# First block of a two-block model on one core: feed-forward part joined to the output projection, its row divisor applied to the products

## What is computed

```python
merged = g_a * (y_a @ w_o_rwkv) + g_b * (y_b @ w_o_att)
h = h + merged @ w_out

z = rmsnorm(h, norm2_g) @ w_ffn_in
z_gate, z_up = jnp.split(z, 2, axis=-1)
h = h + (jax.nn.silu(z_gate) * z_up) @ w_ffn_out
```

## Time and profile before

| | us |
|---|---|
| median of 3 runs | 1678.6 (1671.26 to 1678.84) |
| profiled execution, its own time | 1683.73 |
| its span in the trace | 1681.9 |

### The profile page before, as it was taken

One profiled execution on the slowest core, in us unless ns is written; L12 is line 12 of the kernel. 1 busy time (PEld: TensorE's weight loads), 2 busy tenths in 40 slices (PEclk: granted clock), 3 DMA queues, 4 the chain that ended last, 5 costly groups with the idle time before them and its releaser, 6 DMA issues. The chain is left out here.

```text
span 1681.9 us, 37220 instructions
## 1 busy us (share of the span) xinstructions
PE 1539.9 (92%) x15430; PEld 1247.0 (74%) x15430; DVE 923.8 (55%) x1100; ACT 761.4 (45%) x936; POOL 119.8 (7%) x66
## 2 busy tenths in 40 slices
PE   5998999988998969999999988889999898999996
PEld 4997877888998969999888778866555555555552
DVE  3487434355443356764500433566787676777774
ACT  2346216324442328732111324324676666666663
POOL 0321400001342000000300000000000000000000
PEclk8999999998999989999999999999999999999998
DMA  7556357542554525554022233447999999999992
GB/s 231 166 173 211 115 175 230 190 159 92 188 175 150 178 75 175 163 163 127 28 76 75 76 100 101 133 176 245 404 409 378 354 377 403 408 408 372 408 392 106
DMA packets 197323, 360.10 MB, mean 214 GB/s; under 512 B 12221, under 2 KB 140586, under 8 KB 197034
## 3 DMA queue, kind: packets, MB, share of 16 engines
q1 hardware_dynamic: 197162, 357.82, 60.0%
HBM read 355.03 MB, written 1.05 MB: 212 GB/s over the span
## 5 line engine op out<-in xcount | busy, mean ns | idle before, releaser
L350 PE MATMUL psum<-proj_r 128*128 128x256 f32 x1504 | 380.3, 291 | 34.5 <-DVE proj_r L335 18.7
L351 PE MATMUL psum<-proj_r 128*128 128x256 f32 x1504 | 377.7, 289 | 0.0
L319 DVE TENSOR_TENSOR ring_r<-ring,proj_r 128x2048 fp32r<-128x2048 f32 x94 | 220.6, 2346 | 209.6 <-ACT proj_r L314 208.8
L350 PEld LDWEIGHTS psum<-proj_r 128*128 128x128 f32 x1504 | 299.0, 199 | 38.8 <-issue 28.8
L351 PEld LDWEIGHTS psum<-proj_r 128*128 128x128 f32 x1504 | 298.9, 199 | 0.0
L2191 DVE COPY ring<-proj 128x2048 f32 x189 | 226.9, 1224 | 118.5 <-PE psum L2833 62.9
L314 ACT ACTIVATE proj_r<-ring 128x2048 fp32r<-128x2048 f32 x94 | 179.4, 1908 | 120.9 <-PE psum L354 120.6
L354 PE MATMUL psum<-proj_r,ring_r 128*128 128x256 f32 x1504 | 197.2, 284 | 2.7 <-DVE ring_r L319 2.6
L1661 ACT ACTIVATE ring<-proj 128x1024 f32 x188 | 191.3, 1050 | 14.4 <-issue 8.5
L354 PEld LDWEIGHTS psum<-proj_r,ring_r 128*128 128x128 f32 x1504 | 188.7, 193 | 3.1 <-DVE ring_r L319 3.1
L427 PE MATMUL psum<-u,ring 128*128 128x256 f32 x512 | 124.9, 390 | 6.1 <-ACT proj L1495 6.1
(11 more groups left out here) (495 smaller groups left out, 2256.2 us busy)
## 6 DMA issues: line engine op xcount, KB each, us to landing
ring<-in_w_in SPq DMA_DIRECT2D x65, 1024.0 KB, 5.3
proj<-in_w_exp_gate SPq DMA_DIRECT2D x128, 512.0 KB, 7.6
proj<-in_w_exp_up SPq DMA_DIRECT2D x128, 512.0 KB, 10.1
proj<-in_w_exp_down SPq DMA_DIRECT2D x128, 512.0 KB, 8.4
ring<-in_w_ada SPq DMA_DIRECT2D x24, 1024.0 KB, 7.8
ring<-in_w_ffn_in SPq DMA_DIRECT2D x22, 1024.0 KB, 5.1
ring<-in_w_ffn_out SPq DMA_DIRECT2D x11, 1024.0 KB, 4.9
ring<-in_w_out SPq DMA_DIRECT2D x8, 1024.0 KB, 4.9
```

What stands on the lines that cost most here:

```text
L319: dve.tensor_tensor(ring_r[:, at.slot, :], ring[:, at.slot, :], self.heads[at.buffer].bitcast(F32), ALU.subtract) \
L350: pe.matmul(dst, w, xh, start=start, stop=False, skip_group_check=True)
L351: pe.matmul(dst, w, xl, start=False, stop=False, skip_group_check=True)
```

## The change

- The barrier and the norm stage between output projection and feed-forward go. As soon as chunk 4 + i has added to two tiles of `h`, ACT copies their heads with the gain (`h * g`, not divided by the norm) and squares them, and DVE makes the rests (`head_of_pair`, `rest_of_pair`). The first feed-forward chunk is treated as a ninth chunk of the projection.
- PE sums the squares of a pair of tiles behind chunks 5, 6 and 7 and behind the first feed-forward chunk (`sum_of_pair`); that chunk waits for the rows' rests at four places in place of two.
- The divisor `rs`, one number per token, is applied to the products: DVE multiplies the gate product in PSUM by it (`scale_gate`), ACT applies SiLU in place in SBUF, DVE multiplies by the up product and then again by `rs` (`up_product`). Pair 0 lies in banks 1 and 3 and is written out ahead of the loop.
- Each pair therefore counts twice in `pair_evacuated`. PE asks for the pair two before its own in place of three.
- PE's 14 modulation turns move: 10 ahead of output chunk 0, 4 behind chunk 3.
- A down chunk waits for the split of its own pair alone.

Arguments such as `finished` are passed as functions; names of signals are renumbered to fit.

```diff
--- before.py
+++ after.py
@@ -344,8 +344,8 @@
             for i, (o, (xh, xl), dst, start, stop) in enumerate(products):
-                if halves and i in (0, len(products) // 2):
-                    pe.wait_ge(*reached("input_rests", halves[i > 0]))
+                if halves and i % (len(products) // len(halves)) == 0:
+                    pe.wait_ge(*reached("input_rests", halves[i * len(halves) // len(products)]))
...
@@ -960,9 +960,15 @@
                         act.activation(o.mix.xh[i], merged[:, 4 * i:4 * i + 4, :], ACT.Copy).then_inc(sig("input_heads"), 1)
+                if finished and c >= chunks - 2:
+                    finished(c - (chunks - 2), at(c - 2))
+            if finished:
+                o.mix.head(act, at(chunks))
+                finished(2, at(chunks - 2))
+                finished(3, at(chunks - 1))
...
-        def dve_out(dve, place, o, chunks, first_gated, write, early=0, gates=False):
+        def dve_out(dve, place, o, chunks, first_gated, write, early=0, gates=False, finished=None):
...
@@ -973,8 +979,10 @@
             for c in range(chunks):
-                if c + 1 < chunks:
+                if c + 1 < chunks or finished:
                     o.mix.rest(dve, at(c + 1))
+                if finished and c > chunks - 4:
+                    finished(c - 1 - (chunks - 4))
...
@@ -992,9 +1000,11 @@
                     write(c - (chunks - 4), at(c)).then_inc(evacuated, 1)
+            if finished:
+                finished(3)
...
-        def pe_out(pe, place, o, first_tiles, chunks):
+        def pe_out(pe, place, o, first_tiles, chunks, finished=None):
...
@@ -1009,6 +1019,8 @@
                 multiply_split(pe, sp_, at, products, halves)
+                if finished:
+                    finished(c - (chunks - 3))
...
@@ -1279,12 +1291,11 @@
             st.end()
-            st.end()
...
             for i in range(DFF // CH):
-                pool.wait_ge(*reached("pair_evacuated", i + 4))
-                pool_split(pool, *(flat_of(ap) for ap in (ffn_tmp[i % 3], ffn_h[:, 2 * i:2 * i + 2, :], ffn_l[:, 2 * i:2 * i + 2, :])))
+                pool.wait_ge(*reached("pair_evacuated", 2 * (i + 3)))
+                pool_split(pool, *(flat_of(ap) for ap in (ffn_tmp[(i + 2) % 3], ffn_h[:, 2 * i:2 * i + 2, :], ffn_l[:, 2 * i:2 * i + 2, :])))
...
@@ -1466,21 +1477,32 @@
             place.skip(8 - GATES_FIRST)
-            act_out(act, place, out_1, 8)
-            st.end()
-            act_norm(act, 1)
-            split_free.act_input(act, 1)
-            split_free.head(act, Chunk(place, 0, 0, None))
-            def silu_gate(at):
+            def head_of_pair(i, at):
+                act.wait_ge(evacuated, at.linear + 3)
+                for k in (2 * i, 2 * i + 1):
+                    ins = act.activation(split_free.tiles(k)[0], h[:, k, :], ACT.Copy, scale=v("norm2_g", k))
+                ins.then_inc(sig("input_heads"), 1)
+                act.activation(squares[:, 2 * i:2 * i + 2, :], h[:, 2 * i:2 * i + 2, :], ACT.Square).then_inc(sig("squares_act_1"), 1)
+            act_out(act, place, out_1, 8, finished=head_of_pair)
+            split_free.head(act, Chunk(place, 1, 1, None))
+            act.activation(small[:, 250:251], const("ones")[:, 0:1], ACT.Sqrt)
+            act.wait_ge(*reached("variance_1", 1))
+            act.activation(rs[:, :], rs[:, :], ACT.Sqrt).then_inc(sig("root_1"), 1)
+            split_free.head(act, Chunk(place, 2, 2, None))
+            def silu_gate(pair, buffer):
+                act.wait_ge(*reached("gate_steps", pair * 2 + 1))
+                act.activation(ffn_tmp[buffer], ffn_tmp[buffer], ACT.Silu).then_inc(sig("gate_steps"), 1)
+            def head_and_gate(at):
...
                 if at.j % 2 == 0:
-                    act.wait_ge(multiplied, at.n + 1)
-                    act.wait_ge(*reached("hid_split", at.pair + 1))
-                    src = bank[at.j // 2 % 3 * 2].rearrange("p (m t) -> p m t", t=S)
-                    act.activation(ffn_tmp[at.j // 2 % 3], src, ACT.Silu).then_inc(sig("gate_silu"), 1)
-            sweep(act, place, 2 * (DFF // CH), silu_gate, linear=False, split=True)
+                    silu_gate(at.pair + 1, at.j // 2 % 3)
+            silu_gate(0, 2)
+            place.skip(2, False, True)
+            sweep(act, place, 2 * (DFF // CH) - 2, head_and_gate, linear=False, split=True)
...
@@ -1868,14 +1890,45 @@
             two_tiles = lambda at: bank[2 * at.parity].rearrange("p (m t) -> p m t", t=S)
+            def rest_of_pair(i):
+                dve.wait_ge(*reached("input_heads", INPUTS_BEFORE["ffn"] + i + 1))
+                for k in (2 * i, 2 * i + 1):
+                    head, rest = split_free.tiles(k)
+                    ins = dve.scalar_tensor_tensor(out=rest, in0=h[:, k, :], scalar=v("norm2_g", k), in1=head.bitcast(F32), op0=ALU.mult, op1=ALU.subtract)
+                ins.then_inc(sig("input_rests"), 1)
+            dve.drain().then_inc(sig("pair_evacuated"), 4)
...
                     lambda c, at: dve.tensor_tensor(merged[:, 4 * c:4 * c + 4, :], wide_tiles(at), proj[:, T_GATE + 4 * c:T_GATE + 4 * c + 4, :], ALU.mult),
-                    lambda c, at: dve.tensor_tensor(h[:, 2 * c:2 * c + 2, :], two_tiles(at), h[:, 2 * c:2 * c + 2, :], ALU.add))
-            st.end()
-            dve.drain().then_inc(sig("pair_evacuated"), 3)
-            dve_norm(dve, link, 1, lambda k: v("norm2_g", k))
-            split_free.dve_input(dve, 1)
-            split_free.rest(dve, Chunk(place, 0, 0, None))
+                    lambda c, at: dve.tensor_tensor(h[:, 2 * c:2 * c + 2, :], two_tiles(at), h[:, 2 * c:2 * c + 2, :], ALU.add),
+                    finished=rest_of_pair)
+            by_token = rs[:, :].rearrange("p (o t) -> p o t", o=1).to_broadcast([P, 2, S])
+            def scale_gate(n, pair, buffer, src):
+                dve.wait_ge(multiplied, n)
+                dve.wait_ge(*reached("hid_split", pair + 1))
+                dve.tensor_tensor(ffn_tmp[buffer], src.rearrange("p (m t) -> p m t", t=S), by_token, ALU.mult).then_inc(sig("gate_steps"), 1)
+            def up_product(n, pair, buffer, src):
+                dve.wait_ge(multiplied, n)
+                dve.wait_ge(*reached("gate_steps", pair * 2 + 2))
+                dst = ffn_tmp[buffer]
+                dve.tensor_tensor(dst, dst, src.rearrange("p (m t) -> p m t", t=S), ALU.mult).then_inc(sig("pair_evacuated"), 1)
+                dve.wait_ge(*reached("pair_evacuated", pair * 2 + 5))
+                dve.tensor_tensor(dst, dst, by_token, ALU.mult).then_inc(sig("pair_evacuated"), 1)
+            first = [Chunk(place, j, j, None) for j in range(2)]
+            split_free.rest(dve, first[1])
+            dve.wait_ge(*reached("square_sum_1", 1))
+            dve.tensor_scalar(rs[:, :], bank[7][:, 0:S], 1.0 / D, 1e-6, ALU.mult, ALU.add).then_inc(sig("variance_1"), 1)
+            dve.wait_ge(*reached("root_1", 1))
+            link(dve.reciprocal(rs[:, :], rs[:, :]))
+            scale_gate(first[0].n + 1, 0, 2, bank[1])
+            split_free.rest(dve, first[1].after())
+            up_product(first[1].n + 1, 0, 2, bank[3])
+            place.skip(2, False, True)
...
@@ -1892,15 +1945,11 @@
-            def up_product(at):
+            def rest_and_pair(at):
                 split_free.rest(dve, at.after())
-                if at.j % 2 == 1:
-                    dve.wait_ge(multiplied, at.n + 1)
-                    dve.wait_ge(*reached("gate_silu", at.pair + 1))
-                    dst = ffn_tmp[at.j // 2 % 3]
-                    dve.tensor_tensor(dst, dst, bank[at.j // 2 % 3 * 2 + 1].rearrange("p (m t) -> p m t", t=S), ALU.mult) \
-                       .then_inc(sig("pair_evacuated"), 1)
-            sweep(dve, place, 2 * (DFF // CH), up_product, linear=False, split=True)
+                buffer = at.j // 2 % 3
+                (up_product if at.j % 2 else scale_gate)(at.n + 1, at.pair + 1, buffer, bank[(buffer + 2) % 3 * 2 + at.j % 2])
+            sweep(dve, place, 2 * (DFF // CH) - 2, rest_and_pair, linear=False, split=True)
...
@@ -2493,24 +2542,43 @@
             place.skip(8 - GATES_FIRST)
-            pe_out(pe, place, out_1, 4, 8)
-            st.end()
-            pe_norm(pe, 1)
-            pe.wait_ge(*reached("u_ready", 2 * 2))
+            def turn_mods(first, end):
+                for i in range(first, end):
+                    last = pe.matmul(bank[6][:, 4 * i:4 * i + 4], mod_rows[:, i // 2, i % 2 * P:(i % 2 + 1) * P],
+                                     ident[0:97, :].rearrange("p (q n) -> p q n", n=32)[:, :, 0], start=True, stop=True)
+                return last
+            turn_mods(0, 10)
+            def sum_of_pair(i):
+                pe.wait_ge(*reached("squares_act_1", i + 1))
+                for k in (2 * i, 2 * i + 1):
+                    last = pe.matmul(bank[7][:, 0:S], const("ones"), squares[:, k, :], start=(k == 0), stop=(k == KD - 1))
+                return last
+            def behind_chunk(i):
```

(29 more changed lines are left out.)

16 lines of the change are left out of this document (8 added, 8 removed).

## The result

| | before | after |
|---|---|---|
| median, us | 1678.55 | 1651.78 (4 runs, 1648.34 to 1657.06) |
| span of the profiled execution, us | 1681.9 | 1646.3 |
| stretch from ACT's first copy (L951) to DVE's first addition behind the down products, us | 275.6 | 251.4 |

The changed kernel is faster: ratio 0.9845, 95% interval 0.9806 to 0.9884, or 26.8 us between the medians, where 24.7 were forecast. The two profiled executions differ by 35.6 us. Only 24.2 of them lie in the stretch that was changed; 5.2 lie ahead of it and 6.2 behind, in code that is the same (from the starts and ends of the stretch: 317.4 and 593.0 us before, 312.2 and 563.6 after).

A forecast was written before the change was run, and what follows sets the result against it. PE was taken as the bound, busy 92% of the span, with time to win where it waits or runs at low clock. Terms of -16.3 and -8.45 gave -24.7 us: 1678.6 to 1653.9 us, range 1643 to 1668.

The forecast's parts named there:

- The two holes: Ahead of the first feed-forward chunk and the down products, PE waits or runs at half clock: 25.73 and 14.21 us.
- One sign of the list: PE without idle time of over 0.5 us from the fifth output chunk to the end of the down products.
- The join: Last output chunk to first feed-forward chunk: 6.68 us between third passes in place of 25.73, net -16.3 us.
- All four covers: Last pair of rows, head of chunk 1, divisor and SiLU's table all ready before PE needs them; smallest slack 1.2 us.
- SiLU's and the root's table: ACT's table loads between output projection and feed-forward fall in covered time, 1.28 us each; about 2.66 by the skill.
- The moved turns: Modulation turns ahead of output chunk 0 and behind chunk 3: taken as 0; bounds 1.3 us lost to 5.8 spared.
- The down products: Start of the down chunks: waiting only for their own pair's split makes the distance 5.76 us, not 14.21: -8.45 us.
- What the loop takes on: Feed-forward loop: two more DVE products per pair and a longer gate chain, slack 4.0 us, so cost 0.
- rival (d): The loop's gate chain delays the next gate chunk, making the kernel slower; decides from 4.0 us beyond the count; chance 0.02.
- (a): In the loop, DVE and POOL take turns and each pair could come a microsecond late: +10 us, so 1664; chance 0.07.
- (b): Between output projection and feed-forward a wait stays and PE falls to half clock: 8 us lost, so 1662; chance 0.08.
- (c): The gap ahead of the down products stays, chunk 0 still behind the last split: 1662.3 us; chance 0.04.

The follow-up runs named there:

- the repeats: The changed kernel with no further edit, measured twice more beside the kernel before: 1654.97 us (ratio 0.987) and 1657.19 us (ratio 0.9868).
- the late pair: The changed kernel with two useless ACT copies ahead of the head of the last pair of rows: 1657.88 us, ratio 0.989 to the kernel before.
- the kernel with two copies per pair: The changed kernel with two useless ACT copies of 128x2048 behind SiLU in each loop pair: 1670.57 us, ratio 0.9966 to the kernel before.
- the kernel with one copy per pair: The changed kernel with one useless ACT copy of 128x2048 behind SiLU in each loop pair: 1653.14 us, ratio 0.9864 to the kernel before.

## Why the prediction was right

The forecast was 1653.9 us in a range of 1643 to 1668; measured were 1651.78, and 1654.97 and 1657.19 in the repeats.

- **What bounds the kernel.** The two holes were the places, and both closed. In the loop PE stays the bound, 5.76 us per chunk, and POOL's last split (503.05 to 506.21) runs beside down chunk 0. One sign of the list did not hold as it was written: in the fifth output chunk PE still waits 3.45 us, as it did before (4.33), the turns taking up the difference.
- **The join**, -16.3 by the sum: 25.73 became 6.62 where 6.68 stood, and the other three sums cost 2.58, not 2.77. That is -16.5. All four covers held. The first had 1.0 us of slack, 1.2 by the sum. The sentence "If the 1.2 us fail, only the excess is paid." is wrong: the late pair cost 4.3 us for 2.5 us of waiting.
- **SiLU's and the root's table.** Each load took 1.28 us, as the row had it, in covered time. A drain as in the Trainium skill, "ScalarE: Activation LUTs", section "What ACT_TABLE_LOAD costs", does not show here: the root's load begins 0.02 us after the head ahead of it ends, and the next operation follows it by 0.01. So the switch cost 1.3 us in this trace, not 2.66.
- **The moved turns**, 0 by the sum: they are hidden, and run at 0.12 to 0.15 us. In two of three traces chunk 0 was 0.75 and 0.86 us late, which a kernel without turns there was too. The other end of that bound, that they spare a restart, did not come true: matmuls at half clock follow in both gaps.
- **The down products**, -8.45: 5.76 for 14.21, exactly. Alone, without the new order of banks, 7.41 of it.
- **What the loop takes on**, 0 by the sum: it cost nothing, but the step "PE needs that rest at t + 9.6. Slack 4.0 us" is wrong. The head of the same chunk is due earlier, at t + 5.76, which leaves 2.3 us in the trace, as the kernel with two copies per pair shows. By the same token the point from which rival (d) decides was put 1.7 us too far off. In the first pair only 1.0 us was left, since the small modulation operations held DVE up; the sum did not have them. That the term came out at 0 owes something to luck: in the first pair only a quarter of the slack that was counted on was there.
- **The sum**, -24.7: the stretch has -24.2, -24.1 and -25.2 in three traces, each against the one trace of before. The medians say -26.8, -23.0 and -19.8, so that the first came within 2.1 us of the forecast is partly chance.
- **The rivals.** (a): DVE and POOL do wait for each other, from 409.91 on every second rest of weights takes 2.9 to 3.1 us in place of 2.29, and the chunks stay at 5.76. The product that the change adds (L1920) took its usual 0.69 us, since it stands ahead of POOL's start. The Trainium skill, "SBUF — State Buffer", section "Who interferes with whom", has the second to start blocked fully; the rest at 409.91 began 0.35 us after POOL's product of 1.30 us and took 3.09, within 0.2 us of its usual 2.3 plus the 0.95 that POOL had left. (b), (c) and (d) did not come.

## What to carry to other kernels

Where a norm stands between two matrix stages and its divisor belongs to the token, it can be applied to the products, and the sums can run beside the matmuls; the price is two vector products per pair here, and both were covered. Count a chain's slack to the first thing that the bound engine asks of it, not to the last, and look at the pair with the most other work beside it, not at the usual one. A gap of several microseconds at PE cost its restart at half clock too, 1.6 to 2.9 us here, and 28 small matmuls in the gap did not save that. Compare the stretch that was changed: single executions differed by 10 us and more in code that is the same.

## What was not expected of the hardware

A DVE operation on 128x8 elements took 0.17 us in the kernel before and 1.12 us in the changed one. The line of before:

```profile
393.07 0.17 DVE L1889 TENSOR_SCALAR small<-small 128x8 f32<-128x8 f32 x1
```

The lines of the changed kernel, POOL and DVE:

```profile
386.42 1.29 POOL L1147 TENSOR_TENSOR proj_r<-work,cst 128x512 fp32r<-128x512 f32 x1 [186.24 <-DVE work L1920]
...
386.62 1.12 DVE L1942 TENSOR_SCALAR small<-small 128x8 f32<-128x8 f32 x1
```

It began 0.2 us after a product of POOL and ended when that did. It has a single input tensor, unlike the rest above; the Trainium skill, "SBUF — State Buffer", section "Who interferes with whom", names tensor_scalar among the operations that can take the ports shared with GpSimd, and the row agrees. Two of these stretch a short chain of DVE by 2 us. No chunk waited for it in the changed kernel, but this is the chain ahead of the first pair of the loop: its scaling began 3.54 us after the start of the gate chunk's third pass, 2.21 in the next pair. The 1.33 us are less than the 2 us of the two operations. By these rows the first pair's slack of 1.0 us in place of 2.3, and with it the one wait of the kernel with one copy per pair, go back to two operations of 128x8. This is argued from the rows; no run took the operations out.
